# The residual is added into the PSUM sums inside the expert loop, and the norms behind the loop read PSUM

## The chip, the cores and the metric

The kernel runs on one core of a Trainium2 chip. The metric is device time in microseconds of one execution. Below, PE is TensorE, DVE is VectorE, ACT is ScalarE, POOL is GpSimd and SP is SyncE; "clock" is the clock that TensorE was granted, as a share of 2.4 GHz (1.00 is 2.4 GHz, 0.50 is 1.2 GHz).

## The reference

Two transformer layers over 256 tokens of width 1024, all in float32. Layer 0 has differential attention, layer 1 has latent attention (MLA); each is followed by a layer norm, a mixture of 32 experts of which two are chosen per token, and another layer norm.

```python
def _layernorm(x, g, b):
    mu = jnp.mean(xf, axis=-1, keepdims=True)
    var = jnp.mean(jnp.square(xf - mu), axis=-1, keepdims=True)
    return (xf - mu) * lax.rsqrt(var + NORM_EPS) * g + b
...
def _grouped_moe(x, router_w, router_b, w_gate, w_up, w_down):
    # combine: [tokens, 32], the two gates of each token, zero elsewhere
    for e in range(N_EXPERTS):
        h = jax.nn.silu(t @ w_gate[e]) * (t @ w_up[e])
        y = y + combine[:, e:e + 1] * (h @ w_down[e])
...
for layer in range(DEPTH):
    h = attention(x)
    x = _layernorm(DEEPNORM_ALPHA * x + h, ln_g[layer, 0], ln_b[layer, 0])
    f = _grouped_moe(x, ...)
    x = _layernorm(DEEPNORM_ALPHA * x + f, ln_g[layer, 1], ln_b[layer, 1])
```

## The kernel before

Tokens lie in two tiles of 128 (t = 0, 1), and a tile's 1024 columns in two halves of 512 (c = 0, 1), since one PSUM bank holds 512 float32 per partition. The residual stream is `xs` in SBUF, 128 x 2 x 1024. There are four norms, numbered n = 0 to 3: after attention 0, after experts 0, after attention 1, after experts 1. Each engine has its own program, and semaphores set the order between them; nothing reorders at run time.

**Expert loop** (`moe(l)`, once for each layer). Tokens are sorted by expert on PE with one-hot matmuls, and the experts go in 16 pairs (i = 0 to 15). For a pair PE multiplies a window of 64 tokens for each of the two experts by the gate and up weights, ACT takes silu, DVE multiplies (L1958), PE transposes and multiplies by the down weights into banks 4 and 5. DVE works out the weights of the pair's rows (`weights`, L1934 to L1946, which ends with the semaphore `g_ready`), ACT scales the result with them (`upper`, L1397) and DVE takes the remainder (`lower`, L1950). In the next pair PE adds both parts to the sums of all tokens in banks 0 to 3 (`combine`; bank 2t + c), by accumulating matmuls that `start_sums` (L965) opened with zeros. SP streams the weights of later pairs meanwhile; three slots of SBUF hold them. Between pair 0 and pair 4, DVE and POOL apply the first norm's scale and shift to `xs` (`scale_shift_half`, DVE tile 0, POOL tile 1); until then `xs` holds the normalised value without them.

**Norm behind the loop** (L1494 for n = 1, L1508 for n = 3). When a sum is complete (`sum_ps`, in the order t0c0, t1c0, t0c1, t1c1), DVE adds ALPHA times `xs` to it and writes `xs` (`add`, L1479), takes the statistics of that half (L1482), and so on for four halves, each instruction waiting for the one before. ACT takes the root (L1142), DVE the reciprocal (L1490) and the offset (L1491). For n = 1, ACT normalises tile 0 and the first half of tile 1 (L1146), DVE the second half of tile 1 (L1505). For n = 3, ACT normalises tile 0 and then POOL (640 columns) and DVE (384 columns) apply scale and shift to it, while DVE does tile 1 in two instructions (L1520, L1528); SP then writes each tile to `out` (L556).

**After norm 1** PE transposes `xs` (`transpose_x(2)`, L578) tile by tile, ahead of each tile a few matmuls of zeros that keep PE running while it waits (`keep_clock`, counts `NORM_WAIT`, L574). ACT (L1131) and DVE (L1464) move the transposed tiles to SBUF with scale and shift, and PE multiplies by `mla_w_q_a` and `mla_w_kv_a`. POOL and DVE apply scale and shift to `xs` itself from there on.

Of the kernel before, what the change touches and what calls it, by code (L numbers as in the profile page):

```python
# [30 lines left out]
ALU = mybir.AluOpType  # L31
ACT = mybir.ActivationFunctionType
# [24 lines left out]
LOADED_TURNS = 4  # L57
LAST_SPLIT = 640
B_BANKS = (4, 5, 0, 1, 6, 7, 4, 5, 2, 3, 5, 6)
# [5 lines left out]
OUT_BANKS = (6, 7, 0, 1)  # L65
START_WAIT, FIRST_WAIT, NORM_WAIT, TOP_WAIT, SORT_WAIT = 14, 8, (8, 4), 28, 8

# [76 lines left out]
def build(nc, consts, x, diff_w_qkv, diff_lambda, diff_subln_g, diff_w_o, mla_w_kv_a, mla_kv_norm_g, mla_w_kv_b,  # L144
          mla_w_q_a, mla_q_norm_g, mla_w_q_b, mla_w_o, router_w, router_b, moe_w_gate, moe_w_up, moe_w_down,
          ln_g, ln_b, out):
    with ExitStack() as ctx:  # L147
# [48 lines left out]

        psum = ctx.enter_context(nc.psum_tensor("psum", [P, 8, 512], F32))


# [136 lines left out]
        def gb_loaded(l, half=2):  # L336
            return ld_gb, 32 * (3 * l + half + 1)

        def scaled(x_sem, l, half=2):
            return x_sem, 3 * l + half + 1  # L340
# [97 lines left out]
        def _(sp):  # L438
# [113 lines left out]
            load_ln(1)  # L552
            sp.wait_ge(*scaled(x_pool, 1))
            for t in range(TT):
                sp.wait_ge(*scaled(x_dve, 1, 2 + t))
                sp.dma_start(out[0, t * P:(t + 1) * P, :], xs[:, t, :]).then_inc(out_done, 16)  # L556
            sp.wait_ge(out_done, 16 * TT)


        @block.tensor  # L560
        def _(pe):
# [8 lines left out]
            def transpose_x(n):  # L570

                for t in range(TT):
                    if n:
                        keep_clock(NORM_WAIT[t], (4, 2 if n == 1 else 0)[t])  # L574
                        pe.wait_ge(*ln[n - 1]("norm", (1, 3)[t]))
                    for k in range(KD):
                        at_ = (k % 2) * SEQ + t * P
                        last = pe.transpose(psum[:, 4 + k // 2, at_:at_ + P], xs[:, t, k::KD], ident)  # L578
                        if t and k % 2:
                            last.then_inc(xt[n]["ps"], 1)  # L580
                pe.wait_ge(*xt[n]("sb", KD))
# [541 lines left out]
        def _(act):  # L1123
# [20 lines left out]
            def normalise(n, t, cols):  # L1144
                act.wait_ge(*ln[n]("rstd", t + 1))
                act.activation(xs[:, t, cols], xs[:, t, cols], ACT.Identity, scale=ln_rstd[:, t:t + 1],  # L1146
                               bias=ln_nb[:, t:t + 1]).then_inc(ln[n]["norm"], 1)

# [301 lines left out]
            root(3, 0)  # L1450
            normalise(3, 0, slice(0, D))
            root(3, 1)
# [3 lines left out]
        def _(dve):  # L1456
# [50 lines left out]

            def last_layer_norm(ready):  # L1508


                add(3, 0, 0, ready)
                add(3, 0, 1, ready)
                statistics(3, 0)
                add(3, 1, 0, ready)
                scales(3, 0)
                add(3, 1, 1, ready)
                statistics(3, 1)
                dve.wait_ge(*ln[3]("var", 2))
                dve.wait_ge(*gb_loaded(1))
                chain(dve.scalar_tensor_tensor(out=xs[:, 1, :], in0=xs[:, 1, :], scalar=ln_mv[:, 1, 0:1],  # L1520
                                               in1=gb[1][:, 0, :], op0=ALU.subtract, op1=ALU.mult))
                scales(3, 1)
                dve.wait_ge(*ln[3]("norm", 1))
                cols = slice(LAST_SPLIT, D)
                chain(dve.tensor_tensor(xs[:, 0, cols], xs[:, 0, cols], gb[1][:, 0, cols], ALU.mult))  # L1525
                dve.tensor_tensor(xs[:, 0, cols], xs[:, 0, cols], gb[1][:, 1, cols], ALU.add).then_inc(x_dve, 1)  # L1526
                dve.wait_ge(*ln[3]("rstd", 2))
                dve.scalar_tensor_tensor(out=xs[:, 1, :], in0=xs[:, 1, :], scalar=ln_rstd[:, 1:2],  # L1528
                                         in1=gb[1][:, 1, :], op0=ALU.mult, op1=ALU.add).then_inc(x_dve, 1)

# [285 lines left out]
            def moe(l):  # L1816
# [136 lines left out]

                def pair(i, s, first=False):
                    dve.wait_ge(*m("s_ready", i + 1))
# [3 lines left out]
                    if not first:  # L1959
                        dve.wait_ge(*m("c_ps", i))  # L1960
                    weights(i, 0, m["g_part"], m["g_ready"], i + l * PAIRS)
                    for c in range(2):
# [5 lines left out]
                scale_shift_half(l, 1)  # L1968
                for_pairs_1_up(dve, pair, (1, (PAIRS - 1) // SLOTS))
                with dve.If(more_windows):  # L1970
# [17 lines left out]
            moe(0)  # L1988
            dve.wait_ge(*scaled(x_pool, 0, 1))
            layer_norm(1, lambda t, c: dve.wait_ge(*mo[0]("sum_ps", 2 * c + t + 1)))  # L1990
            mla_attention()
            layer_norm(2, lambda t, c: dve.wait_ge(wo_ps, 4 + 2 * t + c + 1))
            moe(1)
            dve.wait_ge(*scaled(x_pool, 1, 1))
            last_layer_norm(lambda t, c: dve.wait_ge(*mo[1]("sum_ps", 2 * c + t + 1)))


        @block.gpsimd
        def _(pool):
# [134 lines left out]

            cols = slice(0, LAST_SPLIT)
            pool.wait_ge(*ln[3]("norm", 1))
            pool.wait_ge(*gb_loaded(1))
            chain(pool.tensor_tensor(xs[:, 0, cols], xs[:, 0, cols], gb[1][:, 0, cols], ALU.mult))
            pool.tensor_tensor(xs[:, 0, cols], xs[:, 0, cols], gb[1][:, 1, cols], ALU.add).then_inc(x_pool, 1)


# [20 lines left out]
```

## Time and profile before

| | us |
|---|---|
| median of 3 runs (lowest, highest) | 743.93 (740.16, 747.05) |
| the profiled execution's own time | 746.22 |
| its span, first to last instruction | 744.3 |
| PE busy | 694.9 (93%) |
| DVE busy | 333.0 (45%) |
| ACT busy | 214.3 (29%) |
| POOL busy | 137.5 (18%) |
| mean granted clock of PE | 0.977 |

How to read it: the span is attention 0 (to about 133 us), norm 0 and experts 0 (to 377 us), norm 1 and MLA (to 484 us), norm 2 and experts 1 (to 728 us), and the last norm with the output (to 744 us). DVE, ACT and POOL are idle for much of the expert loops, and their share of the span says little about the short stretches between them. In the profile's lists a "group" names the line, the engine, the operation, and what it writes and reads; "idle before" is the idle time of that engine just ahead of it and what ended it.

### The profile page before, as it was taken

How to read it: one execution, taken by the hardware profiler on the slowest of the kernel's cores; microseconds unless marked ns; L12 is line 12 of the kernel's file. 1: busy time of each engine (PE TensorE's matmuls, PEld its weight loads, DVE VectorE, ACT ScalarE, POOL GpSimd, SP SyncE). 2: the span in 40 equal slices, each digit the busy share in tenths (PEclk: the TensorE clock that was granted, in tenths of full speed). 3: DMA queues.
4: the chain of work that ended last, by engine and by line, in shares of the span. 5: the costliest groups of instructions: out<-in, count | busy, mean ns of one | idle time of the engine just before them, and what ended most of it. 6: DMA issues, size and time to landing. Idle time of an engine off the chain costs nothing. (4 is left out here: it accounts for less than half of the span.)

```text
span 744.3 us, 10149 instructions
## 1 busy us (share of the span) xinstructions
PE 694.9 (93%) x3658; PEld 392.6 (53%) x3658; DVE 333.0 (45%) x673; ACT 214.3 (29%) x419; POOL 137.5 (18%) x147
## 2 busy tenths in 40 slices
PE   7999899879999999999979898987999999999992
PEld 5989788444434343345536887845333434344540
DVE  4746754762332324233264557376343323323237
ACT  3668462412111111111144248131221111111112
POOL 6003010141201010011009560105120101010002
PEclk9999999999999999999989999999999999999997
DMA  9980039838999999999994019292999999999981
GB/s 310 385 315 1 1 130 423 356 144 305 422 422 420 421 422 422 422 422 420 423 414 174 0 63 422 88 379 100 357 420 421 421 422 422 422 422 421 420 337 58
DMA packets 40215, 237.65 MB, mean 319 GB/s; under 512 B 3808, under 2 KB 4240, under 8 KB 15088
## 3 DMA queue, kind: packets, MB, share of 16 engines
q1 hardware_dynamic: 39264, 235.64, 77.7%
q10 hardware_dynamic: 576, 1.05, 0.5%
q0 software_dynamic: 336, 0.44, 0.3%
q8 instruction: 25, 0.41, 0.2%
q14 instruction: 14, 0.11, 0.0%
HBM read 236.06 MB, written 1.05 MB: 319 GB/s over the span
## 5 line engine op out<-in xcount | busy, mean ns | idle before, releaser
L563 PE MATMUL psum<-ring,work 128*64 128x512 f32 (+2 forms) x1296 | 234.1, 512 | 7.2 <-DVE work L1923 7.2
L563 PEld LDWEIGHTS psum<-ring,work 128*64 128x64 f32 (+1 forms) x1296 | 95.4, 140 | 143.1 <-issue 119.7
L563 PE MATMUL psum<-ring,scratch 128*64 128x512 f32 x512 | 116.9, 598 | 3.7 <-ACT scratch L1408 3.7
L2031 POOL COPY work<-work 128x512 f32 x60 | 39.1, 654 | 315.9 <-PE psum L563 299.7
L1958 DVE TENSOR_TENSOR scratch<-psum,scratch 128x256 f32<-128x256 f32 x32 | 13.6, 425 | 184.8 <-ACT scratch L1404 184.8
L1397 ACT ACTIVATE x_T_rounded<-psum,small 128x512 fp32r<-128x512 f32 x64 | 44.0, 689 | 108.8 <-DVE scratch_rounded L1946 73.6
L563 PEld LDWEIGHTS psum<-ring,scratch 128*64 128x64 f32 x512 | 33.9, 136 | 68.8 <-issue 63.6
L1404 ACT ACTIVATE scratch<-psum 128x256 f32<-128x256 f32 x32 | 12.3, 385 | 196.2 <-PE psum L563 196.2
L563 PE MATMUL psum<-ring_rounded 128*128 128x256 f32 (+1 forms) x214 | 66.0, 309 | 0.0
L563 PE MATMUL psum<-ring_rounded,x_T_rounded 128*128 128x512 f32 x192 | 60.8, 398 | 1.0 <-DVE work_rounded L1794 0.9
L563 PE MATMUL psum<-x_T_rounded,scratch_rounded 128*128 128x512 f32 x128 | 56.7, 443 | 0.9 <-issue 0.7
L563 PE MATMUL psum<-x_T_rounded,ring_rounded 128*128 128x256 f32 x256 | 48.5, 287 | 1.4 <-DVE work L1573 1.4
L563 PEld LDWEIGHTS psum<-ring_rounded 128*128 128x128 f32 x214 | 41.3, 193 | 2.2
L563 PE MATMUL psum<-zeros_b 128*128 128x512 bf16 x138 | 38.8, 437 | 3.8 <-DVE ring_rounded L1563 2.6
L563 PEld LDWEIGHTS psum<-x_T_rounded,ring_rounded 128*128 128x128 f32 x256 | 40.5, 192 | 1.8 <-DVE work L1573 1.6
L563 PEld LDWEIGHTS psum<-x_T_rounded,scratch_rounded 128*128 128x128 f32 x128 | 24.2, 189 | 30.4 <-issue 27.6
L563 PEld LDWEIGHTS psum<-ring_rounded,x_T_rounded 128*128 128x128 f32 x192 | 35.5, 188 | 8.6 <-DVE work_rounded L1794 1.1
L1950 DVE SCALAR_TENSOR_TENSOR work_rounded<-psum,small,x_T_rounded 128x512 fp32r<-128x512 f32 x32 | 24.0, 751 | 28.1 <-ACT x_T_rounded L1397 28.1
L1937 DVE SCALAR_TENSOR_TENSOR scratch<-x_T,cst 128x256 f32<-128x256 f32 x32 | 15.8, 493 | 40.9 <-PE psum L563 40.9
L1950 DVE SCALAR_TENSOR_TENSOR scratch_rounded<-psum,small,x_T_rounded 128x512 fp32r<-128x512 f32 x32 | 24.0, 751 | 19.1 <-ACT x_T_rounded L1397 18.9
L1593 DVE TENSOR_TENSOR ring_rounded<-ring,ring_rounded 128x1024 fp32r<-128x1024 f32 x20 | 24.1, 1253 | 6.2 <-ACT ring_rounded L1186 6.1
L563 PEld LDWEIGHTS psum<-zeros_b 128*128 128x128 bf16 x138 | 14.6, 112 | 23.0 <-issue 9.2
(252 smaller groups left out, 889.7 us busy)
## 6 DMA issues: line engine op xcount, KB each, us to landing
ring<-in_moe_w_gate SPq DMA_DIRECT2D x64, 1024.0 KB, 15.5
ring<-in_moe_w_up SPq DMA_DIRECT2D x64, 1024.0 KB, 19.7
ring<-in_moe_w_down SPq DMA_DIRECT2D x64, 1024.0 KB, 20.2
ring<-in_diff_w_qkv SPq DMA_DIRECT2D x5, 2048.0 KB, 19.6
ring<-in_diff_w_o SPq DMA_DIRECT2D x1, 4096.0 KB, 14.5
ring<-in_mla_w_o SPq DMA_DIRECT2D x1, 4096.0 KB, 35.6
ring<-in_mla_w_q_b SPq DMA_DIRECT2D x1, 2304.0 KB, 29.3
ring<-in_mla_w_kv_b SPq DMA_DIRECT2D x1, 2048.0 KB, 28.1
```

The costliest lines, as they stand in the source:

```text
L563: return pe.matmul(dst, lhsT, rhs, start=start, stop=stop, skip_group_check=True)
L1397: act.activation(y_hi[:, c * 512:(c + 1) * 512], psum[:, 4 + c, :], ACT.Copy, scale=gate_col)\
L1404: act.activation(act_s, psum[:, 6, 0:FF], ACT.Silu).then_inc(m["s_ready"], 1)
L1593: dve.tensor_tensor(qkv_chunk(ring_r, c)[:, :, cols], qkv_chunk(ring, c)[:, :, cols], w_hi[:, c % 2, :, cols], ALU.subtract).then_inc(w_lo ...
L1937: dve.scalar_tensor_tensor(out=comb, in0=key_row[:, 0, :], scalar=at_, in1=gate_row[:, 0, :], op0=ALU.is_equal, op1=ALU.mult).then_inc(par ...
L1950: dve.scalar_tensor_tensor(out=y_lo[c], in0=psum[:, 4 + c, :], scalar=gate_col, in1=y_hi[:, c * 512:(c + 1) * 512], op0=ALU.mult, op1=ALU. ...
L1958: dve.tensor_tensor(h_sb, psum[:, 6, FF:2 * FF], act_s, ALU.mult).then_inc(m["h_ready"], 1)
L2031: last = pool.tensor_copy(xg[:, buf, :, j * WIN:(j + 1) * WIN], xsT[:, :, bass.ds(a, WIN)])
```

## The change

Four edits. (1) In pairs 4 to 7 of both expert loops DVE adds ALPHA times one half of `xs` to its bank of the sums, in PSUM (`residual`), between its wait for the previous pair's combination (`c_ps`) and the weights of the pair. (2) Norm 1 takes its statistics from the banks and normalises from them; the four additions behind the loop are gone, and all four statistics come ahead of the first reciprocal. (3) Norm 3 does the same, and applies everything on DVE: two instructions from PSUM, then tile 0 in one and tile 1 in two halves, the output leaving in three transfers instead of two; ACT's and POOL's parts, and the waits for them on DVE and SP, are gone. (4) The zero matmuls ahead of the transposes behind norm 1 become 11 and 0 instead of 8 and 4.

```diff
-LAST_SPLIT = 640
+RESIDUAL_PAIR = 4
...
-START_WAIT, FIRST_WAIT, NORM_WAIT, TOP_WAIT, SORT_WAIT = 14, 8, (8, 4), 28, 8
+START_WAIT, FIRST_WAIT, TOP_WAIT, SORT_WAIT = 14, 8, 28, 8
+NORM_WAIT = {1: (8, 4), 2: (11, 0), 3: (8, 4)}
...
+        sums = psum[:, 0:2 * TT, :].rearrange("p (t c) n -> p t (c n)", t=TT)
...  # SP, output
-            sp.wait_ge(*scaled(x_pool, 1))
-            for t in range(TT):
-                sp.wait_ge(*scaled(x_dve, 1, 2 + t))
-                sp.dma_start(out[0, t * P:(t + 1) * P, :], xs[:, t, :]).then_inc(out_done, 16)
-            sp.wait_ge(out_done, 16 * TT)
+            for n, (t, cols) in enumerate(((0, slice(0, D)), (1, slice(0, 512)), (1, slice(512, D)))):
+                sp.wait_ge(*scaled(x_dve, 1, 2 + n))
+                sp.dma_start(out[0, t * P:(t + 1) * P, cols], xs[:, t, cols]).then_inc(out_done, 16)
+            sp.wait_ge(out_done, 16 * 3)
...  # PE, transpose_x
-                        keep_clock(NORM_WAIT[t], (4, 2 if n == 1 else 0)[t])
+                        keep_clock(NORM_WAIT[n][t], (4, 2 if n == 1 else 0)[t])
...  # ACT, normalise
-                act.activation(xs[:, t, cols], xs[:, t, cols], ACT.Identity, scale=ln_rstd[:, t:t + 1],
+                act.activation(xs[:, t, cols], sums[:, t, cols] if n == 1 else xs[:, t, cols], ACT.Identity,
...  # ACT, end
             root(3, 0)
-            normalise(3, 0, slice(0, D))
             root(3, 1)
...  # DVE, norms (last_layer_norm before is replaced)
+            def sum_statistics(n):
+                def part(t, c):
+                    dve.wait_ge(*mo[n // 2]("sum_ps", 2 * c + t + 1))
+                    chain(dve.bn_stats(ln_stats[:, t, c, :], psum[:, 2 * t + c, :]))
+                part(0, 0)
+                part(1, 0)
+                part(0, 1)
+                statistics(n, 0)
+                part(1, 1)
+                scales(n, 0)
+                statistics(n, 1)
+            def sum_layer_norm(n):
+                sum_statistics(n)
+                scales(n, 1)
+                dve.wait_ge(*ln[n]("rstd", 2))
+                dve.tensor_scalar(xs[:, 1, D // 2:], sums[:, 1, D // 2:], ln_rstd[:, 1:2], ln_nb[:, 1:2], ALU.mult,
+                                  ALU.add).then_inc(ln[n]["norm"], 1)
+            def last_layer_norm():
+                sum_statistics(3)
+                dve.wait_ge(*gb_loaded(1))
+                dve.wait_ge(*ln[3]("var", 2))
+                for t in range(TT):
+                    dve.scalar_tensor_tensor(out=xs[:, t, :], in0=sums[:, t, :], scalar=ln_mv[:, t, 0:1],
+                                             in1=gb[1][:, 0, :], op0=ALU.subtract, op1=ALU.mult)\
+                       .then_inc(ln[3]["norm"], 1)
+                dve.wait_ge(*ln[3]("rstd", 1))
+                dve.wait_ge(*ln[3]("norm", 1))
+                dve.scalar_tensor_tensor(out=xs[:, 0, :], in0=xs[:, 0, :], scalar=ln_rstd[:, 0:1],
+                                         in1=gb[1][:, 1, :], op0=ALU.mult, op1=ALU.add).then_inc(x_dve, 1)
                 scales(3, 1)
                 dve.wait_ge(*ln[3]("rstd", 2))
+                dve.wait_ge(*ln[3]("norm", 2))
+                for c in range(2):
+                    cols = slice(c * 512, (c + 1) * 512)
+                    dve.scalar_tensor_tensor(out=xs[:, 1, cols], in0=xs[:, 1, cols], scalar=ln_rstd[:, 1:2],
+                                             in1=gb[1][:, 1, cols], op0=ALU.mult, op1=ALU.add).then_inc(x_dve, 1)
...  # DVE, expert loop
-                def pair(i, s, first=False):
+                def residual(t, c):
+                    cols = slice(c * 512, (c + 1) * 512)
+                    dve.wait_ge(*scaled((x_dve, x_pool)[t], l, c))
+                    dve.scalar_tensor_tensor(out=sums[:, t, cols], in0=xs[:, t, cols], scalar=ALPHA,
+                                             in1=sums[:, t, cols], op0=ALU.mult, op1=ALU.add)
+                def pair(i, s, first=False, sum_part=None):
...
                         dve.wait_ge(*m("c_ps", i))
+                    if sum_part is not None:
+                        residual(*sum_part)
                     weights(i, 0, m["g_part"], m["g_ready"], i + l * PAIRS)
...
-                for_pairs_1_up(dve, pair, (1, (PAIRS - 1) // SLOTS))
+                for n in range(2 * SLOTS):
+                    i = RESIDUAL_PAIR + n
+                    pair(i, i % SLOTS, sum_part=(n // 2, n % 2) if n < 4 else None)
+                for_pairs_1_up(dve, pair, (3, (PAIRS - 1) // SLOTS))
...
             moe(0)
-            dve.wait_ge(*scaled(x_pool, 0, 1))
-            layer_norm(1, lambda t, c: dve.wait_ge(*mo[0]("sum_ps", 2 * c + t + 1)))
+            sum_layer_norm(1)
...
             moe(1)
-            dve.wait_ge(*scaled(x_pool, 1, 1))
-            last_layer_norm(lambda t, c: dve.wait_ge(*mo[1]("sum_ps", 2 * c + t + 1)))
+            last_layer_norm()
...  # POOL, end
-            cols = slice(0, LAST_SPLIT)
-            pool.wait_ge(*ln[3]("norm", 1))
-            pool.wait_ge(*gb_loaded(1))
-            chain(pool.tensor_tensor(xs[:, 0, cols], xs[:, 0, cols], gb[1][:, 0, cols], ALU.mult))
-            pool.tensor_tensor(xs[:, 0, cols], xs[:, 0, cols], gb[1][:, 1, cols], ALU.add).then_inc(x_pool, 1)
```

## Rows read from the trace of the kernel before

**Rows 1.** The page: busy us (share of the span) and instructions.
```profile
PE 694.9 (93%) x3658; PEld 392.6 (53%) x3658; DVE 333.0 (45%) x673; ACT 214.3 (29%) x419; POOL 137.5 (18%) x147
```

**Rows 2.** The chain of waits, its end: start us, us, what.
```profile
728.73 0.69 DVE x_res L1479
...
735.14 0.24 issue
...
737.57 0.17 DVE ln_rstd L1490
...
737.98 1.37 DVE x_res L1525
...
739.93 1.20 DVEq L147
```

**Rows 3.** Groups by form, 728 to 744 us: count, busy us, mean ns, idle before.
```profile
L1482 DVE BATCH_NORM_STATS2 ln_stats<-x_res 128x6 f32<-128x512 f32 x4 | 2.8, 694 | 0.1
L1479 DVE SCALAR_TENSOR_TENSOR x_res<-x_res,psum 128x512 f32<-128x512 f32 x4 | 2.7, 669 | 0.0
...
L1528 DVE SCALAR_TENSOR_TENSOR x_res<-x_res,ln_rstd,work 128x1024 f32<-128x1024 f32 x1 | 1.3, 1277 | 0.0
```

**Rows 4.** Timeline of pair 3 of the first expert loop: start us, us, instruction.
```profile
217.23 0.69 ACT L1397 ACTIVATE x_T_rounded<-psum,small 128x512 fp32r<-128x512 f32 x1 [2.77 <-DVE scratch_rounded L1946]
219.34 0.75 DVE L1950 SCALAR_TENSOR_TENSOR scratch_rounded<-psum,small,x_T_rounded 128x512 fp32r<-128x512 f32 x1 [0.63 <-ACT x_T_rounded L1397]
225.36 0.50 PE L563 MATMUL psum<-x_T_rounded,scratch_rounded 128*128 128x512 f32 x1
```

**Rows 5.** Timeline of PE alone around norm 1.
```profile
378.60 1.90 PE L563 MATMUL psum<-zeros_b 128*128 128x512 bf16 x8
383.70 1.97 PE L578 MATMUL psum<-cst,x_res 128*128 128x128 f32 x8 [3.19 <-ACT x_res L1146]
385.46 1.91 PE L563 MATMUL psum<-zeros_b 128*128 128x512 bf16 x4
387.17 1.91 PE L578 MATMUL psum<-cst,x_res 128*128 128x128 f32 x8
390.22 1.24 PE L563 MATMUL psum<-ring,x_T 128*128 128x384 f32 x3 [1.14 <-DVE x_T L1464]
```

**Rows 6.** Timeline of DVE and ACT in norm 1.
```profile
377.53 0.69 DVE L1479 SCALAR_TENSOR_TENSOR x_res<-x_res,psum 128x512 f32<-128x512 f32 x1
...
382.40 1.24 ACT L1146 ACTIVATE x_res<-x_res,ln_neg_mean_rstd,ln_rstd 128x1024 f32<-128x1024 f32 x1 [1.43 <-DVE ln_neg_mean_rstd L1491]
...
383.97 0.30 ACT L1142 ACTIVATE ln_sd<-ln_mean_var,eps 128x1 f32<-128x1 f32 x1 [0.33 <-DVE ln_mean_var L1485]
...
384.75 0.82 ACT L1146 ACTIVATE x_res<-x_res,ln_neg_mean_rstd,ln_rstd 128x512 f32<-128x512 f32 x1 [0.48 <-DVE ln_neg_mean_rstd L1491]
```

**Rows 7.** Windows: us, busy PE, PEld, DVE, ACT, POOL, PEclk, DMA share, GB/s.
```profile
381.00:382.00 1.00, 0.00 (x0) 0.00 (x0) 0.93 (x3) 0.00 (x0) 0.00 (x0) 1.00 0.99 406
383.00:384.00 1.00, 0.30 (x2) 0.30 (x3) 0.90 (x2) 0.67 (x2) 0.00 (x0) 0.50 1.03 428
389.00:390.00 1.00, 0.08 (x1) 0.00 (x0) 1.00 (x3) 1.00 (x3) 0.68 (x1) 0.72 1.01 406
...
414.00:415.00 1.00, 1.00 (x3) 0.75 (x3) 1.00 (x1) 0.00 (x0) 1.00 (x1) 0.50 0.00 0
```

**Rows 8.** Timeline of PE alone behind norm 2, where the clock was 1.00.
```profile
487.54 1.16 PE L578 MATMUL psum<-cst,x_res 128*128 128x128 f32 x8
490.24 1.07 PE L563 MATMUL psum<-x_T,work 128*32 128x256 f32 x16 [1.55 <-DVE x_T L1464]
```

**Rows 9.** DMA issues: count, KB each, median us from issue to landing.
```profile
ring<-in_mla_w_q_b SPq DMA_DIRECT2D x1, 2304.0 KB, 29.3
...
out_x<-x_res SPq DMA_DIRECT2D x2, 512.0 KB, 2.7
```

**Rows 10.** Timeline of SP, the issue of `mla_w_q_b`.
```profile
356.06 2.14 SPq L535 DMA_DIRECT2D ring<-in_mla_w_q_b  x1
```

More of the change, by code:

```diff
@@ L1145, in normalise @@
                 act.wait_ge(*ln[n]("rstd", t + 1))
-                act.activation(xs[:, t, cols], xs[:, t, cols], ACT.Identity, scale=ln_rstd[:, t:t + 1],
-                               bias=ln_nb[:, t:t + 1]).then_inc(ln[n]["norm"], 1)
+                act.activation(xs[:, t, cols], sums[:, t, cols] if n == 1 else xs[:, t, cols], ACT.Identity,
+                               scale=ln_rstd[:, t:t + 1], bias=ln_nb[:, t:t + 1]).then_inc(ln[n]["norm"], 1)
             def layer_norm(n):
@@ L1506, in layer_norm @@
                                   ALU.add).then_inc(ln[n]["norm"], 1)
[L1508 to L1517, printed above, removed]
-                dve.wait_ge(*ln[3]("var", 2))
-                dve.wait_ge(*gb_loaded(1))
-                chain(dve.scalar_tensor_tensor(out=xs[:, 1, :], in0=xs[:, 1, :], scalar=ln_mv[:, 1, 0:1],
-                                               in1=gb[1][:, 0, :], op0=ALU.subtract, op1=ALU.mult))
+            def sum_statistics(n):
[9 more added lines that the diff above has]
+                statistics(n, 1)
@@ L1522, in last_layer_norm @@
                 scales(3, 1)
[L1523 to L1526, printed above, removed]
                 dve.wait_ge(*ln[3]("rstd", 2))
-                dve.scalar_tensor_tensor(out=xs[:, 1, :], in0=xs[:, 1, :], scalar=ln_rstd[:, 1:2],
-                                         in1=gb[1][:, 1, :], op0=ALU.mult, op1=ALU.add).then_inc(x_dve, 1)
+                dve.wait_ge(*ln[3]("norm", 2))
```

## The prediction

> **What bounds the kernel now.** The page first: PE is busy 93% of the span [rows 1], so what counts is the 7% in which it is not, and PE work done at the lower clock. The chain of waits says where that lies: inside both expert loops it is PE alone, and from 728.73 us to the end it is DVE, one instruction after the other, up to 741.13 (739.93 + 1.20), then the output transfer [rows 2]. That tail is the first place where the change can pay. The second is norm 1, in the timeline of PE: the zero matmuls end at 380.50, the transposes of tile 0 start at 383.70 on a release by ACT, and the product with `mla_w_q_a` starts at 390.22 [rows 5]. In the windows the clock is still 1.00 in 381 to 382 with PE stopped, 0.50 (1.2 GHz) in 383 to 384, and partly back (0.72) in 389 to 390 [rows 7]. So the eight transposes of each tile take 1.97 and 1.91 us and the four zero matmuls 1.91 [rows 5]; behind norm 2, at 1.00, eight transposes take 1.16 [rows 8].
>
> **Part 1, the residual in the loop.** Four more DVE instructions per loop, each between `c_ps` and the weights of its pair. No row shows DVE writing PSUM. Below, the same operation reading PSUM and writing SBUF takes 0.67 on average [rows 3]; above, I allow twice that, 1.4; I take 0.7, the row being the same operation on as many elements. Queued behind it are the weights, `g_ready`, ACT's two scalings and DVE's two remainders. ACT's first scaling already waits for the weights (idle 2.77 until L1946 is done), so the whole 0.7 passes on. But the second remainder ends at 219.34 + 0.75 = 220.09 and PE wants it at 225.36 [rows 4]: 5.3 us of cover against 0.7, or 1.4. The semaphores for scale and shift were raised by pair 3. The same loop body now runs straight through for six pairs, which costs DVE nothing that this cover doesn't hide. **0 on the path.** If the cover were gone, each of eight instructions would cost 0.7, 5.6 in all.
>
> **Part 2, norm 1.** Before, DVE starts at 377.53 and ACT gets the factors of tile 0 at 382.40 [rows 6], 4.87 us later: three additions, three statistics, the aggregate, and reciprocal and offset (0.41 for the two, 737.57 to 737.98 in rows 2). After, four statistics: 4 x 0.72 (0.69 and a step of 0.03) + 0.2 for the aggregate (half of the 0.41) + 0.41 + 0.05 to ACT = 3.54, so ACT starts at 381.07, 1.33 earlier. The fourth sum is complete before its turn: it comes 2.3 us after DVE starts, PE has stopped on the zeros by 378.60.
> ACT reads PSUM now. Bounds for 1024 columns: 1.24, the SBUF row [rows 6], and 1.11, that less the 0.13 by which 512 columns from PSUM (0.69, rows 4) undercut 512 from SBUF (0.82, rows 6). I take 1.11: PE gets tile 0 at 382.23. Eleven zero matmuls at the 0.24 of [rows 5] end at 381.2, ahead of that, so they hold nothing up, and PE stands still for 1.0 us instead of 3.2. The clock then stays at 1.00, as it did for longer than that in [rows 7]; the transposes end at 383.4 (1.16, rows 8).
> Tile 1: ACT's root takes 0.30 from 382.2, 0.48 more pass until ACT can normalise [rows 6], and its half takes 0.69 from PSUM: ready at 383.65, with DVE's half alongside. With no zeros ahead, PE goes at 383.7 instead of 387.17. From there to the product it took 2.70 at full clock (487.54 to 490.24, rows 8), where DVE's moves, not PE, are last: 386.4 instead of 390.22. **-3.8 us.** What was hidden comes closer: `mla_w_q_b` lands at 356.06 + 29.3 = 385.4 [rows 9, 10], and ACT, which splits it next, is free at 386.2 (0.8 to spare). POOL's and DVE's scale and shift and all of MLA follow from the transposes, and with them the reload of the slots by SP, so the gain travels unchanged to the second loop.
>
> **Part 3, norm 3.** Before, 728.73 to 741.13: 12.40 us [rows 2]. After: four statistics 2.88, aggregate 0.2, reciprocal and offset 0.41, second aggregate 0.2, wait 0.24 (the "issue" of rows 2), two instructions of 1024 from PSUM at 1.28 each, tile 0 in 1.28 [rows 3], reciprocal and offset 0.41, two halves at 0.69 and 0.03 less the last step, 1.41: 9.59. ACT's normalisation and POOL's two instructions leave nothing that anyone waits for. So -2.8. From PSUM the 1024 columns have no row: 1.28 (SBUF) below, 2 x 0.75 (L1950, rows 4) above, which would give back 0.4. Then the output: the last transfer has 256 KB, not 512. 512 KB took 2.7 [rows 9]. Half the bytes take 1.35 at least, if time goes by bytes alone, and 2.7 at most, if by none; I take 2.4, nearer to the upper end, since the two transfers of before, 1.2 us apart, took the same 2.7 beside each other, so that little of it is the moving of bytes. **-0.3, together -3.1 us.** Three issues on SP instead of two cost nothing: they are over 0.7 us apart.
>
> One thing speaks against the change. In [rows 3] the addition with a PSUM operand takes 0.67 and the statistics from SBUF 0.69, for 512 elements each: PSUM is no dearer. The Trainium skill ("VectorE: DVE Perf Modes", section "The TRN2 errata — SBUF-src ops pay a fixed extra latency per instruction") gives a VectorE instruction that reads PSUM 62 cycles more than one that reads SBUF. By that the eleven DVE instructions that now read PSUM outside the loops would return an estimated 0.7 us in all, the sum being 6.2; I go by the row.
>
> **Sum.** 3.8 + 3.1 = 6.9. The profiled execution took 746.22 (span 744.3 and 1.9 around it), which gives 739.3. That execution was 2.3 above the median of 743.93, and I apply the same saving to the median: 743.93 - 6.9 = **737.0**.
>
> **Rivals.**
> *A, the clock.* The low stretch is in the trace of one execution; the median one may have lost less there, or the changed kernel may drop as well: behind the transposes PE waits 1.5 us for the moves [rows 8], and only dense work comes after it. Without the drop before, the gain of norm 1 is 1.4 + 0.5 of saved zeros = 1.9. Total 5.0: 738.9. For it: the runs before spread over 6.9 us. Against: PE stands for 3.2 us in every run.
> *B, a later low stretch goes too.* In 414 to 415 the clock is 0.50 with PE full [rows 7], after PE had waited between small transposes; it lasted about 3.4 us, so 1.7 were lost. With the work ahead at full clock it may not fall. Total 8.6: 735.3. Nothing in the change touches that wait.
> *C, norm 1's gain is caught by something that did not move.* The only candidate with little slack is `mla_w_q_b`, 0.8 us; behind it POOL, which waits for the transposes, sets the pace of the split. If the whole 3.8 went there: 740.8.
> *D, slower: DVE from PSUM.* If statistics and the like cost twice as much from PSUM as from SBUF, four statistics are 2.8 longer at both norms, ACT is kept waiting until PE has stood long enough for the clock to fall again, and the two wide instructions add 2.6: norm 1 gives 0.3, the tail costs 2.2 net: 745.8. It decides from about 0.6 us more per 512 elements. Against: the addition reads PSUM at 0.67.
> *E, the change doesn't do what it says*: the four additions cost the loop as much as they saved behind it (5.6 above): 742.6. The 5.3 us of cover speak against it.
>
> **Chances.** Forecast 0.45, A 0.24, B 0.12, C 0.08, D 0.04, E 0.04, something unseen 0.03. The range 733.0 to 741.3 takes in A, B and C, the bounds of ACT's and DVE's times (0.3 and 0.4, and the transfer's), and a median of three that moves by some 2 us. About 1% is what a measurement of this kernel can tell from no change, and 1% is 7.4 us, just beyond the forecast's 6.9: faster by over 1% takes all of B and under half of the forecast's own spread, 0.42; within 1% is 0.54; slower by over 1% needs D with more on top, 0.04.
>
> **What would show it.** In the profile of the changed kernel: statistics from PSUM at 0.69; residual additions near 0.7 in pairs 4 to 7 and PE without a gap there; ACT starting 3.5 us after DVE at norm 1, the clock at 1.00 until the product with `mla_w_q_a`, and 8.8 us (377.5 to 386.4) from DVE's start to it instead of 12.7; 9.5 us of DVE in the tail, and the last transfer under 2.7. I am wrong if PE waits in the loop, if the clock falls between the transposes and that product, or if the stretch from product to second loop grows by what norm 1 gave.

## The result, and the profile after

| | before | changed |
|---|---|---|
| median of 20 runs (us) | 744.54 | 736.95 |
| lowest run (us) | 739.52 | 735.09 |
| ratio to before, 95% interval | | 0.9903 (0.9881 to 0.9924) |
| profiled execution: own time, span (us) | 746.22, 744.3 | 735.09, 733.3 |
| mean granted clock of PE in it | 0.977 | 0.988 |

The changed kernel is faster by 1.0%, about 7.2 us by the ratio (5.7 to 8.9 by its interval) and 7.6 between the medians; 6.9 was forecast, and 737.0 us against 736.95 measured. One of the changed kernel's 20 runs took 1015.73 us at a mean clock of 0.651; the ratio, and what is said below of spread and mean clock, go by its other 19 runs, whose median is 736.87. The two profiled executions lie 11.0 us apart, more than the medians: the one of before is slower than its median, the one of the changed kernel is its fastest run. So the two traces can be compared stretch by stretch, but not in sum. Each line of the table starts where the one above it ends.

| stretch (us) | before | changed |
|---|---|---|
| start to DVE's first instruction at norm 1 | 377.53 | 375.57 |
| from there to the product with `mla_w_q_a` | 12.69 | 8.89 |
| from there to DVE's first instruction at norm 2 | 77.64 | 79.36 |
| from there to DVE's first instruction at norm 3 | 260.87 | 257.79 |
| norm 3 on DVE | 12.40 | 9.07 |
| last DVE instruction to the end | 3.17 | 2.62 |

Norm 1, the timeline of PE alone in the changed kernel (start us, us, instruction), which answers to [rows 5]:

```profile
376.81 2.55 PE L564 MATMUL psum<-zeros_b 128*128 128x512 bf16 x11
380.27 1.16 PE L579 MATMUL psum<-cst,x_res 128*128 128x128 f32 x8 [0.91 <-ACT x_res L1147]
381.75 1.16 PE L579 MATMUL psum<-cst,x_res 128*128 128x128 f32 x8 [0.32 <-DVE x_res L1527]
384.46 5.83 PE L564 MATMUL psum<-ring,x_T 128*128 128x384 f32 x12 [1.55 <-DVE x_T L1464]
```

PE stands for 0.91 us ahead of tile 0 instead of 3.19, and the transposes take 1.16 us instead of 1.9. DVE and ACT in the same stretch, to be read against [rows 6]:

```profile
375.57 2.15 DVE L1512 BATCH_NORM_STATS2 ln_stats<-psum 128x6 f32<-128x512 f32 x3
...
379.01 1.21 ACT L1147 ACTIVATE x_res<-psum,ln_neg_mean_rstd,ln_rstd 128x1024 f32<-128x1024 f32 x1 [0.71 <-DVE ln_neg_mean_rstd L1491]
380.12 0.28 ACT L1143 ACTIVATE ln_sd<-ln_mean_var,eps 128x1 f32<-128x1 f32 x1
...
380.88 0.78 ACT L1147 ACTIVATE x_res<-psum,ln_neg_mean_rstd,ln_rstd 128x512 f32<-128x512 f32 x1 [0.48 <-DVE ln_neg_mean_rstd L1491]
380.88 0.81 DVE L1527 TENSOR_SCALAR x_res<-psum,ln_rstd,ln_neg_mean_rstd 128x512 f32<-128x512 f32 x1
```

ACT starts 3.44 us after DVE (4.87 before). But the clock fell a little later than in [rows 7], in windows with the same columns (the third number from the end is the clock):

```profile
384.00:385.00 1.00, 0.54 (x2) 0.41 (x3) 1.00 (x2) 1.00 (x2) 1.00 (x1) 0.99 0.96 401
385.00:386.00 1.00, 1.00 (x3) 0.46 (x2) 1.00 (x1) 1.00 (x2) 0.92 (x2) 0.50 1.04 430
386.00:387.00 1.00, 1.00 (x3) 0.64 (x2) 0.96 (x2) 1.00 (x2) 1.00 (x1) 0.50 1.04 426
387.00:388.00 1.00, 1.00 (x3) 0.39 (x3) 1.00 (x1) 1.00 (x1) 1.00 (x1) 0.50 0.94 377
388.00:389.00 1.00, 1.00 (x4) 0.67 (x3) 1.00 (x1) 0.63 (x2) 1.00 (x2) 0.80 1.04 418
```

From 385 to 388.4 the dense product runs at 1.2 GHz with PE full. That is why the third stretch of the table is 1.7 us longer than before. From DVE's start at norm 1 to norm 2 the two traces are 90.33 and 88.25 us long: of the 3.8 us of norm 1, 2.1 are left. (Both traces have one more low stretch behind it, [rows 7] and 408 to 413 us.)

Norm 3, the timeline of DVE at the end of the changed kernel:

```profile
724.93 0.20 DVE L1485 BATCH_NORM_AGGREGATE ln_mean_var<-ln_stats 128x2 f32<-128x12 f32 x1
725.23 2.48 DVE L1536 SCALAR_TENSOR_TENSOR x_res<-psum,ln_mean_var,work 128x1024 f32<-128x1024 f32 x2
727.62 1.28 DVE L1541 SCALAR_TENSOR_TENSOR x_res<-x_res,ln_rstd,work 128x1024 f32<-128x1024 f32 x1
728.82 0.16 DVE L1490 RECIPROCAL ln_rstd<-ln_sd 128x1 f32<-128x1 f32 x1
...
729.26 1.42 DVE L1548 SCALAR_TENSOR_TENSOR x_res<-x_res,ln_rstd,work 128x512 f32<-128x512 f32 x2
```

DVE starts at 721.61 and ends at 730.68; the first 3.62 us are the four statistics and the small instructions. Nothing runs on POOL. The groups that answer to [rows 3] and to the open prices (count, then least, median and most ns, first and last start in us, form):

```profile
L1482 DVE BATCH_NORM_STATS2 ln_stats<-x_res x8: 694/695/695, 124.8 to 480.9; 128x6 f32<-128x512 f32 x8
...
L1512 DVE BATCH_NORM_STATS2 ln_stats<-psum x8: 644/694/699, 375.6 to 723.9; 128x6 f32<-128x512 f32 x8
...
L1978 DVE SCALAR_TENSOR_TENSOR psum<-x_res,psum x8: 696/696/697, 226.3 to 610.9; 128x512 f32<-128x512 f32 x8
...
L1536 DVE SCALAR_TENSOR_TENSOR x_res<-psum,ln_mean_var,work x2: 1276/1280/1284, 725.2 to 726.4; 128x1024 f32<-128x1024 f32 x2
```

Statistics cost the same from PSUM (694 ns) as from SBUF (695), and an addition that reads and writes PSUM takes 696.

### The profile page after: what moved, and what is told of

Same layout as the page of the kernel before. It is cut to its first block and busy times, and to the rows that moved or that the text cites. A ratio compares the mean times of both kernels' runs of the same rounds, so it can differ in the third digit from the quotient of the medians.

```text
span 733.3 us, 10061 instructions
## 1 busy us (share of the span) xinstructions
PE 688.5 (94%) x3657; PEld 389.5 (53%) x3657; DVE 330.9 (45%) x674; ACT 212.5 (29%) x418; POOL 133.0 (18%) x145
## 5 line engine op out<-in xcount | busy, mean ns | idle before, releaser
L564 PE MATMUL psum<-zeros_b 128*128 128x512 bf16 x137 | 34.1, 400 | 3.8 <-DVE ring_rounded L1583 2.6
L564 PE MATMUL psum<-work_rounded,scratch_rounded 128*128 128x512 f32 x64 | 25.3, 396 | 0.0
## 6 DMA issues: line engine op xcount, KB each, us to landing
ring<-in_moe_w_gate SPq DMA_DIRECT2D x64, 1024.0 KB, 15.5
ring<-in_mla_w_q_b SPq DMA_DIRECT2D x1, 2304.0 KB, 29.5
```

What stands on the lines that cost most here:

```text
L564: return pe.matmul(dst, lhsT, rhs, start=start, stop=stop, skip_group_check=True)
```

## The experiments

Three theories were at stake. **The chain theory**, the prediction's: DVE's additions behind the loops were on the path, are not in the loops, and the two norms gain separately. **The counts theory**: the zero matmul counts, through the clock, carry norm 1's gain. **The luck theory**: much of the difference is where the clock falls, which changes from run to run. In the edits below `...` stands for lines left out; a quoted paragraph is what was expected of the run, and "rival" in it is another outcome and what it would mean. Runs of one group share the runs of the kernel before on the same chip. A "low stretch" is one in which the granted clock is 0.50; those seen here are about 3.4 us long, and one of twice that counts as two.

### One half of the change at a time

`tail_only`: norm 1, the first loop and the counts as before.

```diff
-                    pair(i, i % SLOTS, sum_part=(n // 2, n % 2) if n < 4 else None)
+                    pair(i, i % SLOTS, sum_part=(n // 2, n % 2) if n < 4 and l == 1 else None)
-NORM_WAIT = {1: (8, 4), 2: (11, 0), 3: (8, 4)}
+NORM_WAIT = {1: (8, 4), 2: (8, 4), 3: (8, 4)}
-            sum_layer_norm(1)
+            dve.wait_ge(*scaled(x_pool, 0, 1))
+            layer_norm(1, lambda t, c: dve.wait_ge(*mo[0]("sum_ps", 2 * c + t + 1)))
```

(ACT's `normalise` reads `xs` again.)

> The new norm 3 with its residual additions in the second expert loop; norm 1, the first loop and the zero matmul counts (8, 4) as before. Theory (the saved DVE chain): the stretch from DVE's first instruction behind the second loop to the end of the span is 11.7 us as in the changed kernel (15.6 before), norm 1 keeps its 12.7 us from DVE's start to the product with mla_w_q_a when the clock falls there, and the whole is 3.5 to 4 us faster than before, ratio about 0.995. Rival (the gain is clock luck and zero counts): no faster than before, ratio 1.000.

Measured: median 740.32, ratio 0.9948 (0.9920 to 0.9976), 3.9 us by the ratio. In its trace norm 1 takes 12.69 us as before and the tail 11.68 (9.07 on DVE and 2.61). The chain theory holds for norm 3, and in size too. The run takes all edits of norm 3 together; how they share the 3.9 us is read from the traces alone: 3.33 on DVE, 0.55 behind it.

`mid_only`: the other half; the last norm, ACT's and POOL's part of it and the output as before.

```diff
-                    pair(i, i % SLOTS, sum_part=(n // 2, n % 2) if n < 4 else None)
+                    pair(i, i % SLOTS, sum_part=(n // 2, n % 2) if n < 4 and l == 0 else None)
-            last_layer_norm()
+            dve.wait_ge(*scaled(x_pool, 1, 1))
+            last_layer_norm(lambda t, c: dve.wait_ge(*mo[1]("sum_ps", 2 * c + t + 1)))
```

> The new norm 1 with its residual additions in the first expert loop and zero counts (11, 0); the last norm and the output as before. Theory: 8.9 us from DVE's start at norm 1 to the product with mla_w_q_a, tail 15.6 us, the whole 2 to 4 us faster than before (3.8 by the two profiles, less where the clock falls a little later on dense work), ratio 0.995 to 0.997. The two halves alone add up to the whole (0.990). Rival (something shared, such as the counts or the loop, makes the gain): the halves don't add up.

Measured: median 742.50, ratio 0.9989 (0.9957 to 1.0020). Its trace shows the 8.89 us at norm 1 and the 15.57 of the tail; the ratio gives 0.8 us, with an interval from 3.2 faster to 1.5 slower, and the medians, 744.71 and 742.50, lie 2.2 us apart. By the ratio that is less than the 2 us expected, though the interval reaches it; by the ratios, too, the halves (3.9 and 0.8) don't add up to the whole (7.2), which was the rival's sign, but the intervals are too wide to tell. So the stretch is won, and the runs don't show how much of it reaches the total. Windows of this kernel behind norm 1:

```profile
384.00:388.00 4.00, 3.16 (x6) 1.82 (x7) 3.96 (x4) 4.00 (x5) 3.92 (x2) 0.66 1.00 413
408.00:412.00 4.00, 3.13 (x9) 2.48 (x9) 3.49 (x15) 0.84 (x2) 1.30 (x1) 0.65 0.01 2
```

Two low stretches lie on dense work there, as in the changed kernel, and the stretch from the product to norm 2 takes 79.31 us; in `tail_only`, where the clock fell only ahead of the product, it took 76.07. Halves measured like this don't settle norm 1's worth.

### The zero matmul counts

`after_zeros_8_4`: the changed kernel with the old counts.

```diff
-NORM_WAIT = {1: (8, 4), 2: (11, 0), 3: (8, 4)}
+NORM_WAIT = {1: (8, 4), 2: (8, 4), 3: (8, 4)}
```

> The changed kernel with 8 and 4 zero matmuls ahead of the transposes behind norm 1 instead of 11 and 0. Theory (the shorter DVE chain carries the gain): PE stands 1.6 us instead of 0.9 ahead of tile 0, the four zeros of 0.22 each fit between tile 0 and tile 1 but for some 0.6 us; the stretch of norm 1 is 9.5 us against 8.9, the whole within 1 us of the changed kernel, ratio 0.990 to 0.992. Rival (the counts carry it, by the clock): the clock is at 0.50 for the transposes as before, the stretch is over 11 us, ratio 0.994 or more.

Measured: median 736.25, ratio 0.9903 (0.9872 to 0.9935), the same as the changed kernel. PE in its trace:

```profile
376.90 1.90 PE L564 MATMUL psum<-zeros_b 128*128 128x512 bf16 x8
380.37 1.16 PE L579 MATMUL psum<-cst,x_res 128*128 128x128 f32 x8 [1.56 <-ACT x_res L1147]
381.36 1.03 PE L564 MATMUL psum<-zeros_b 128*128 128x512 bf16 x4
382.22 1.04 PE L579 MATMUL psum<-cst,x_res 128*128 128x128 f32 x8
```

The stretch is 9.15 us (9.5 expected), and the clock was 1.00 all the way to norm 2 (76.04 us). The counts of the change are worth 0.26 us in that stretch, which the runs cannot see; the counts theory falls for the changed kernel.

`before_zeros_11_0`: the kernel before with the new counts, indexed by norm as in the change.

```diff
-START_WAIT, FIRST_WAIT, NORM_WAIT, TOP_WAIT, SORT_WAIT = 14, 8, (8, 4), 28, 8
+... NORM_WAIT ... = ... {1: (8, 4), 2: (11, 0), 3: (8, 4)} ...
```

> The kernel before with 11 and 0 zero matmuls ahead of the transposes behind norm 1, nothing else. Theory: PE stands 2.5 us instead of 3.2; tile 1 starts when it is normalised (385.6 instead of 387.2 at the same clock), so at least 0.5 and at most 2 us less at norm 1, ratio 0.997 to 0.999. Rival (the counts carry the gain of norm 1): 3 to 4 us less, ratio 0.995 or less.

Measured: median 742.72, ratio 0.9983 (0.9952 to 1.0014). In the trace:

```profile
380.19 2.55 PE L563 MATMUL psum<-zeros_b 128*128 128x512 bf16 x11
385.28 1.16 PE L578 MATMUL psum<-cst,x_res 128*128 128x128 f32 x8 [2.54 <-ACT x_res L1146]
387.20 1.16 PE L578 MATMUL psum<-cst,x_res 128*128 128x128 f32 x8 [0.76 <-ACT x_res L1146]
389.91 2.52 PE L563 MATMUL psum<-ring,x_T 128*128 128x384 f32 x7 [1.55 <-DVE x_T L1464]
```

This is the old DVE chain at full clock: 10.79 us from DVE's first instruction (379.12) to the product. It splits the 3.8 us of norm 1: 12.69 to 10.79 is the clock and the four zeros that held tile 1, 10.79 to 8.89 is the shorter chain. PE stood 2.54 us here and its clock stayed at 1.00, where it fell in 3.19 us of standing in [rows 5]; that is one trace of each, and whether the new counts always keep the clock in the kernel before is not shown.

### How much the loop covers

`residual_plus_4` and `residual_plus_12`: behind each residual addition 4 (12) more of 0 times the residual into the same bank, one after the other, which leave the values as they are.

```diff
-                    dve.scalar_tensor_tensor(out=sums[:, t, cols], in0=xs[:, t, cols], scalar=ALPHA,
-                                             in1=sums[:, t, cols], op0=ALU.mult, op1=ALU.add)
+                    for a in (ALPHA,) + (0.0,) * 4:
+                        chain(dve.scalar_tensor_tensor(out=sums[:, t, cols], in0=xs[:, t, cols], scalar=a,
+                                                       in1=sums[:, t, cols], op0=ALU.mult, op1=ALU.add))
```

> The changed kernel with four more additions of 0 times the residual into the same bank, one after the other, behind each of the four residual additions of each loop: 3.5 us instead of 0.6 ahead of the weights in pairs 4 to 7. Theory (5.3 us of cover in each pair): PE has no gap in the loops, the two stretches with the loops are as long as in the changed kernel. Rival (the additions are on the path in part): 8 times up to 2.9 us more, 23 us.

Measured: 738.95 in one run. Forty additions of 695 ns, and PE's three largest waits are those of the changed kernel (7.2, 4.7 and 3.7 us against 7.1, 4.7 and 3.7). The last is the only one inside the loops: eight waits of 0.46 us for an ACT copy, in pairs 0, 13, 14 and 15 of each, and the kernel before has the same eight. PE never waits for DVE's remainders. From norm 2 to norm 3 it took 257.80 us against 257.79, and from pair 0's first matmul to norm 1 213.73 against 213.72; the longer total comes from ahead of that, where the additions are not (low stretches at 84 and 142 us). The residual additions cost nothing on PE's path.

> The same with twelve more additions each: 9.3 us ahead of the weights. Theory (5.3 us of cover): PE waits about 4 us in each of the eight pairs, 32 us in all (28 to 36), time near 769. Rival (the cover is larger, since other waits of the pair move along): under 20 us; rival (no cover): 70 us.

Measured: 778.40 in one run, 9 us more than the theory's 769. The waits of PE (what it waited for: us in total, times, longest us), and two windows behind such waits:

```profile
PE psum L564 <- DVE scratch_rounded L1970: 27.8, 8, 3.9
```

```profile
244.00:248.00 4.00, 4.00 (x14) 2.20 (x15) 0.96 (x2) 0.38 (x1) 0.00 (x0) 0.59 1.01 420
260.00:264.00 4.00, 3.08 (x8) 2.46 (x9) 1.15 (x3) 0.60 (x2) 0.00 (x0) 0.62 1.02 424
```

The eight waits are there, 3.5 us each for thirteen additions that take 9.45, so the cover is 9.45 - 3.5 = 6.0 us, not 5.3; their sum of 27.8 lies just under the 28 to 36 expected. The rest of the 43 us (776.6 - 733.3), 15.5, fits the clock: it fell behind such waits, in the first loop in 244 to 248 and 260 to 264, and the dense work of the pair then ran at 1.2 GHz. This trace has eleven more low stretches than the changed kernel's, ten of them behind these waits; at 1.65 us each (the price found below on dense work) they come to an estimated 18 us. Here a wait of PE cost more than its length.

### Holding the clock

`fill_moves`: six zero matmuls behind the transposes of norm 1, where PE waits 1.55 us for the moves.

```diff
+                if n == 2:
+                    keep_clock(6, 0)
                 pe.wait_ge(*xt[n]("sb", KD))
```

> The changed kernel with six more zero matmuls on PE behind the transposes of norm 1, in the 1.5 us in which it waits for the moves to SBUF. Theory (in the changed kernel's trace the clock fell to 0.50 in 384 to 388 us, behind the two short stands of PE and the transposes, and cost 1.7 us on the dense product): the clock stays at 1.00 there, DVE's start to the product stays 8.9 us or grows by 0.1, and the stretch from the product to norm 2 takes 77.7 us or less instead of 79.4; ratio to before 0.987 to 0.990. Rival (the fall there is tied to something else): the stretch stays 79.4 and the ratio 0.990.

Measured: median 735.51, ratio 0.9879 (0.9839 to 0.9919). The stretch from the product to norm 2 is 77.67 us, with one low stretch (407 to 411) instead of two. As expected, but the runs don't tell it from the changed kernel, and `after_zeros_8_4` had no low stretch there without any fill, so that this one trace doesn't show what the six zeros do. This execution was the slowest of its six (739.42 us), with four low stretches around norm 2 (486 to 493 and 510 to 517), where nothing was filled.

`fill_all`: the same at norms 0, 1 and 2, and in the other stands of PE around which the clock had fallen.

```diff
+                if n:
+                    keep_clock(6, 0)
                 pe.wait_ge(*xt[n]("sb", KD))
...  # MLA, last transposes of the norms
+                keep_clock(4, 7)
                 pe.wait_ge(mq["c_ready"], 4)
...
+                keep_clock(3, 7)
                 pe.wait_ge(mq["w_lo"], 3)
...  # ahead of the first pair of each expert loop
+                pe.wait_ge(*m("sort_act", 1))
+                keep_clock(12, 0)
                 pair(0, 0, 0, True)
```

> The changed kernel with zero matmuls in every stand of PE ahead of which or behind which its clock fell in the traces so far: six behind the transposes of norms 0, 1 and 2, four and three around the last transposes of the MLA norms, twelve ahead of pair 0 of each expert loop. Nothing else is changed. Theory (low-clock stretches on dense work, 3.4 us each and 1.7 us of cost, make the spread of the runs and hide part of norm 1's gain): the mean granted clock of all runs is 0.990 or more, the runs spread over less than 3 us, the median is 3 to 6 us below the changed kernel's 737, ratio 0.982 to 0.986. Rival (the zeros delay PE where it was needed, or falls come elsewhere): the ratio is 0.989 or more.

Measured: median 731.89 (729.70 to 733.32), ratio 0.9832 (0.9793 to 0.9870). The mean clock over its runs is 0.993, against 0.985 in the changed kernel's and 0.981 in those of before. Its six runs spread over 3.6 us; the six of `fill_moves` over 7.7, the changed kernel's 19 over 6.1, those of before (11 and more in a group) over 8.7 to 10.6. PE at norm 1, and the windows in which the changed kernel's clock had fallen:

```profile
383.38 1.16 PE L579 MATMUL psum<-cst,x_res 128*128 128x128 f32 x8 [0.32 <-DVE x_res L1533]
384.38 1.46 PE L564 MATMUL psum<-zeros_b 128*128 128x512 bf16 x6
386.09 4.14 PE L564 MATMUL psum<-ring,x_T 128*128 128x384 f32 x12 [0.25 <-DVE x_T L1470]
```

```profile
385.00:387.00 2.00, 1.75 (x7) 0.84 (x6) 2.00 (x4) 2.00 (x3) 2.00 (x1) 1.00 1.00 418
408.00:412.00 4.00, 3.78 (x18) 2.94 (x17) 3.61 (x10) 1.10 (x3) 2.60 (x1) 1.00 0.01 2
```

The stretch of norm 1 stays 8.88 us, and from the product to norm 2 it is 76.03. By the ratios and their intervals this version beats both kernels. The spread came out 0.6 us wider than expected.

### The change with the clock held in both kernels

`before_filled`: the kernel before with the fills of `fill_all` and `NORM_WAIT` 20 and 0 at norm 1, so that PE stands 0.6 and 0.75 us there. `tail_only_filled`: `tail_only` with the same. `mid_only_filled`: `mid_only` with the fills of `fill_all`. `fill_all_again`: `fill_all`. Beside the edits shown above, the first two have

```diff
+... NORM_WAIT ... = ... {1: (8, 4), 2: (20, 0), 3: (8, 4)} ...
```

> The kernel before with the same zero matmuls in PE's stands as fill_all (6 behind the transposes of norms 0, 1 and 2, 4 and 3 at the MLA norms, 12 ahead of pair 0), and 20 and 0 ahead of norm 1's transposes, so that PE stands there under half a microsecond. Theory (the change is worth 3.9 us in the tail and 1.9 us at norm 1 in bare work, 10.8 to 8.9 us from DVE's start to the product, and the rest of what it gains is clock): 737.5 to 739, ratio 0.991 to 0.993 to the kernel before, 5.5 to 6.5 us above fill_all. Rival (the change's gain is mostly clock): within 4.5 us of fill_all, 736 or less.

> The new norm 3 alone, with the same fills as before_filled (20 and 0 at norm 1). Theory: 3.9 us below before_filled and 1.9 us above fill_all, about 734. Rival (the halves overlap or help each other): not additive, off by over 1 us.

> The new norm 1 alone with the fills of fill_all (11 and 0 at norm 1). Theory: 1.9 us below before_filled and 3.9 us above fill_all, about 736; norm 1 takes 8.9 us from DVE's start to the product. Rival: the new norm 1 gains nothing once the clock is held, equal to before_filled within 0.5 us.

> fill_all once more, beside the other three on one chip: 731 to 733, ratio 0.982 to 0.986 to the kernel before.

| | median (us) | ratio to before | norm 1 | product to norm 2 | norm 3 and output |
|---|---|---|---|---|---|
| before_filled | 738.31 | 0.9898 (0.9854 to 0.9942) | 10.79 | 76.06 | 15.61 |
| tail_only_filled | 734.44 | 0.9843 (0.9800 to 0.9887) | 10.78 | 76.02 | 11.74 |
| mid_only_filled | 734.94 | 0.9856 (0.9813 to 0.9898) | 8.89 | 76.06 | 15.60 |
| fill_all_again | 732.57 | 0.9815 (0.9773 to 0.9858) | 8.88 | 76.06 | 11.69 |

With PE's stands filled, the whole change is worth 738.31 - 732.57 = 5.7 us by the medians (5.5 to 6.5 expected), the tail 3.9 on top of the old norm 1 and 2.4 on top of the new, norm 1 3.4 and 1.9. So the two halves taken alone (3.9 + 3.4) exceed the whole by 1.5 us, which was the recorded rival's sign ("not additive, off by over 1 us"); `mid_only_filled` came 2.4 us above `fill_all_again` where 3.9 was expected. The ratios have intervals of 3 us either way and don't decide it. The traces do for the two stretches: they are worth 1.9 and 3.9 us in every combination, 5.8 in all. What differs besides is at the start of the kernel: the traces of `before_filled` and `tail_only_filled` have one low stretch there, those of the other two have two.

The fills held the clock where they were put. Not counting the fall at the very end, where PE has no work, the five traces with all of them have one or two low stretches, all before 90 us, and none at norm 1, in MLA or in the loops; the other eight, leaving out `residual_plus_12`, have two to seven. The mean clock still differs a little (0.989 in `before_filled`'s runs, 0.992 in `fill_all_again`'s).

The luck theory holds for the difference between the two first profiles. For what the runs gain beyond 5.8 us it is not shown: the 7.2 has an interval from 5.7 to 8.9, and a fall that follows PE's stands at norm 1 is changed by the change itself.

## Why the prediction was right

**The bound and the places.** Both places were named, and both gave: the trace shows the chain of DVE at norm 3 and PE's stand at norm 1 shortened; what else moved is where the clock fell. One reading was too wide: the chain of waits starts at 512.40 us and so shows the second loop only, and there pieces of ACT, and once of DVE, of 0.4 us lie on it in pairs 0 and 13 to 15. The change doesn't touch them.

**Part 1, the loop.** 0 was right: 40 additions for 8 cost nothing, and PE waits for none of them. The addition costs 0.696 us where 0.7 was taken. The cover is 6.0 where 5.3 was worked out, since ACT's second scaling waited 0.70 us for PE anyway and takes that much of a delay.

**Part 2, norm 1.** -3.8 was forecast and 12.69 to 8.89 measured, down to single times: ACT 3.44 us after DVE's start (3.54 forecast), transposes at full clock, 2.71 us from tile 1 to the product (2.70). Two small errors cancel: ACT starts 0.10 earlier, and its 1024 columns take 1.21 from PSUM and not the 1.11 taken. That bound came from an instruction with a scale alone (L1397, 0.69). The trace of before had the form that norm 1 uses, with a scale and a bias for each partition, out of PSUM, at 0.09 us more:

```profile
L1387 ACT ACTIVATE work<-psum,ln_b_cols,ln_g_cols x8: 780/782/784, 156.1 to 510.5; 128x512 f32<-128x512 f32 x8
```

ACT's half of tile 1 took the same 0.78. DVE's half takes 0.81, so that it and not ACT releases PE. What failed is behind the product's start. The clock stayed at 1.00 up to it (384.46 us), as forecast, and fell half a microsecond later; "the gain travels unchanged to the second loop" did not hold: 1.7 us came back on the product, and 2.1 of the 3.8 were left at norm 2. That is the second half of rival A. It was not the bad luck of one execution: of the unfilled traces with the new norm 1 and the new counts all three (the changed kernel, `mid_only`, `residual_plus_4`) have it, with 79.3 to 79.4 us from the product to norm 2, and `after_zeros_8_4`, with the old counts, has not. What was said of the counts, that the eleven zeros hold nothing up, is right; but the gain of norm 1 contains 1.9 us of clock and zeros, most of which the changed kernel has with the old counts as well (9.15 us).

**Part 3, norm 3.** -3.1 was forecast, 15.57 to 11.69 is -3.9. The mis-sized terms: DVE took 9.07 instead of 9.59, because the first aggregate runs beside the statistics behind it (0.12 us between their starts), the wait ahead of the wide instructions was 0.1 us and not 0.24, and what follows a wide instruction starts 0.08 before its end, three times over; and the last transfer, 256 KB, landed in 2.2 us and not 2.4, so the end comes 2.62 after DVE instead of 3.17. Least, median and most of the three transfers to `out` in the changed kernel (the 2.6 is the one of 512 KB):

```profile
DMA to landing us min/median/max: 2.2/2.2/2.6
```

**The rule weighed.** The trace decides for the row: 694 and 695 ns, 1280 and 1277 ns. The Trainium skill ("VectorE: DVE Perf Modes", section "The TRN2 errata — SBUF-src ops pay a fixed extra latency per instruction") has 62 cycles more for a PSUM source; by that the four statistics and the two wide instructions would be longer, and they are not. One instruction is dearer, and the same page of the Trainium skill (section "Why PSUM operands drop a tier") names it: `tensor_scalar` on float32 gets its doubled rate from SBUF only. Here it took 0.55 us from SBUF and 0.81 from PSUM in norm 1. The trace of before had that price as well, eight times, for `tensor_scalar` with two operands for each partition out of PSUM:

```profile
L1916 DVE TENSOR_SCALAR work<-psum,ln_g_cols,ln_b_cols x8: 801/804/810, 159.5 to 513.0; 128x512 f32<-128x512 f32 x8
```

The prediction left this out; it cost under 0.1 us, ACT's half being 0.78.

**The sum.** 6.9 against 7.2 by the ratio. The mechanism was right, but the hit to a tenth is partly luck. As traced, the two parts give 2.1 (DVE's start at norm 1 to norm 2) and 3.9, 6.0 in all: norm 1 brought 1.7 less to norm 2 than forecast and the tail 0.8 more. Bare work is 5.8. The remaining 1 to 1.5 us of the 7.2 is within its interval; that it is clock is likely and not shown. Rival A had norm 1 right: its 1.9 is the bare work there (10.79 to 8.89), and the changed kernel did drop behind the transposes; its total of 5.0 is short by the tail. B's stretch did not go: the clock fell again in 408 to 413. What is missing in the profiled execution of the changed kernel are the low stretches of before at 140, 492 and 515 us, in code that the change leaves alone; that is luck, and makes 5.0 of the 11.0 us between the two profiles. C did not come about, but it was close: `mla_w_q_b` landed at 354.15 + 29.5 = 383.65 and ACT took it up at 384.09, 0.4 us later where 0.8 was forecast. For the load behind it ACT waited 0.37 us, and no matmul waited for ACT in turn:

```profile
388.69 3.70 ACT L1299 CAST ring_rounded<-ring 128x2048 fp32r<-128x2048 f32 x2 [0.37 <-DMA ring<-in_mla_w_kv_b]
```

D and E are refuted by the prices and by the two loop experiments.

## What to carry to other kernels

An addition that ends a loop can go into the loop, on an engine whose result the bottleneck fetches late; read the slack from the instruction that needs it, and test it by multiplying the work until it shows. A gain that is partly clock must be compared with the clock held in both kernels: as they came, the halves measured 3.9 and 0.8 us and the whole 7.2; with PE's stands filled, 3.9, 3.4 and 5.7. Even then the traces, at 3.9, 1.9 and 5.8, say more than six runs of each. When a wait is shortened, look at the next stand of the same engine: here the fall of the clock moved from the transposes, where it and the four zeros cost 1.9 us, onto the dense product, where it cost 1.7. And take a price from the instruction of the same form: the trace of before had both PSUM prices of norm 1 (0.78 and 0.80 us).

## What the runs showed of the hardware

Where the clock falls changes from run to run, and the sum shows in the runs: in the changed kernel's runs a mean clock of 0.988 goes with 735.1 to 736.5 us and 0.977 with 741.14. Each low stretch on dense work cost about 1.65 us (76.06, 77.67 and 79.36 us between the product and norm 2 with none, one and two of them). Short runs of zero matmuls into a free PSUM bank in eight places (three norms, two in MLA, two loops, and norm 1's own count), in time in which PE stood anyway, made the kernel before faster by 1.0% (ratio 0.9898, 0.9854 to 0.9942) without a change to any other engine's program: about as much as the change itself.
